# The new keys' value product in a hybrid attention step: one product of 256 columns for two samples instead of one of 128 for each

## The reference

```
# per sample b: 16 queries x 8 heads = 128 query rows, 128 cached + 16 new latent keys of width 512
s = (q_lat @ ckv.T + q_rope @ krope.T) * (128 + 64) ** -0.5     # all_ckv = concat(past, new)
p = softmax(s)
o_lat = p @ ckv                                                 # 128 x 512: the value product
o_a = o_lat (per head) @ w_uv.T
```

## Time and profile before

| | us |
|---|---|
| median of 3 runs (892.14 to 892.81) | 892.15 |
| profiled execution | 892.28 |
| its span | 890.4 |
| TensorE busy (matmuls) | 866.2 |
| TensorE weight loads (beside the matmuls) | 766.4 |
| VectorE, ScalarE, POOL busy | 437.8, 342.3, 125.8 |

### The profile page before, as it was taken

One profiled execution on the slowest core, in us unless ns is written; L12 is line 12 of the kernel. 1 busy time (PEld: TensorE's weight loads), 2 busy tenths in 40 slices (PEclk: granted clock), 3 DMA queues, 4 the chain that ended last, 5 costly groups with the idle time before them and its releaser, 6 DMA issues.

```text
span 890.4 us, 14063 instructions
## 1 busy us (share of the span) xinstructions
PE 866.2 (97%) x5684; PEld 766.4 (86%) x5684; DVE 437.8 (49%) x903; ACT 342.3 (38%) x634; POOL 125.8 (14%) x207
## 2 busy tenths in 40 slices
PE   3999999999999999999999999999999999999996
PEld 2777778899999988888899989988989998888886
DVE  3524442344744224453455467364465566687272
ACT  5423343244453223422333353332244436554252
POOL 0000003110210000103241300000312123630000
PEclk9999999999999999999999999999999999999998
DMA  9999966855544243447463576555898833894313
GB/s 370 413 413 417 379 241 215 254 195 165 153 147 140 92 148 113 135 157 251 144 200 113 159 280 251 213 190 190 273 324 282 270 102 109 324 267 138 123 60 130
DMA packets 50640, 190.07 MB, mean 213 GB/s; under 512 B 7664, under 2 KB 8296, under 8 KB 45328
## 3 DMA queue, kind: packets, MB, share of 16 engines
q1 hardware_dynamic: 35568, 141.61, 44.8%
q0 software_dynamic: 14864, 47.30, 16.5%
q10 hardware_dynamic: 144, 0.26, 0.1%
HBM read 178.55 MB, written 12.69 MB: 215 GB/s over the span
## 4 chain that ended last, share of the span: by engine, by line
PE 90%; DVE 3%; DMA 3%; ACT 2%; issue 1%; SPq 0%; ACTq 0%; DVEq 0%
PE proj L2049 34%; PE proj L2039 30%; DMA araw<-in_ada_pairs 3%; PE bankO L2020 2%; PE proj L2090 2%; PE bankS L2049 2%; PE proj L2020 2%; PE bankT L2049 2%; PE bankO L2171 1%; PE bankS L2090 1%; PE bankO L2183 1%; PE bankO L2258 1%; PE bankS L2240 1%; PE bankO L2269 1%; PE bankS L2039 1%
## 5 line engine op out<-in xcount | busy, mean ns | idle before, releaser
L1465 DVE TENSOR_TENSOR w_lo<-raw,w_hi 128x1024 fp32r<-128x1024 f32 (+3 forms) x166 | 196.2, 1186 | 209.3 <-ACT w_hi L1076 208.1
L1076 ACT ACTIVATE w_hi<-raw 128x1024 fp32r<-128x1024 f32 (+3 forms) x168 | 168.6, 1006 | 179.9 <-PE proj L2039 93.7
L2049 PE MATMUL proj<-hT_hi,w_hi 128*128 128x384 f32 x576 | 198.0, 344 | 0.0
L2049 PE MATMUL proj<-hT_hi,w_lo 128*128 128x384 f32 x576 | 193.3, 336 | 0.0
L2049 PE MATMUL proj<-hT_lo,w_hi 128*128 128x384 f32 x576 | 193.0, 335 | 0.0
L2039 PE MATMUL proj<-w_hi,hT_hi 128*128 128x512 f32 (+2 forms) x458 | 174.5, 381 | 1.2 <-DVE hT_lo L1543 0.9
L2039 PE MATMUL proj<-w_hi,hT_lo 128*128 128x512 f32 (+2 forms) x458 | 171.5, 374 | 0.0
L2039 PE MATMUL proj<-w_lo,hT_hi 128*128 128x512 f32 (+2 forms) x458 | 171.2, 374 | 0.0
L2049 PEld LDWEIGHTS proj<-hT_hi,w_hi 128*128 128x128 f32 x576 | 108.3, 188 | 8.6 <-issue 7.4
L2049 PEld LDWEIGHTS proj<-hT_lo,w_hi 128*128 128x128 f32 x576 | 108.3, 188 | 0.1
L2049 PEld LDWEIGHTS proj<-hT_hi,w_lo 128*128 128x128 f32 x576 | 108.2, 188 | 0.0
(11 more groups left out here) (399 smaller groups left out, 1178.8 us busy)
## 6 DMA issues: line engine op xcount, KB each, us to landing
raw<-in_units SPq DMA_DIRECT2D x181, 512.0 KB, 4.1
araw<-in_ada_pairs SPq DMA_DIRECT2D x32, 1024.0 KB, 8.6
wuvT<-in_w_uv_t POOLq DMA_DIRECT2D x8, 512.0 KB, 6.5
kcT<-in_dsa_k_t POOLq DMA_DIRECT2D x8, 512.0 KB, 6.1
vc<-in_cache_dsa_v POOLq DMA_DIRECT2D x8, 512.0 KB, 5.3
gate_scratch<-stage POOLq DMA_DIRECT2D x8, 384.0 KB, 4.1
raw<-in_units SPq DMA_DIRECT2D x8, 336.0 KB, 3.7
raw<-in_units SPq DMA_DIRECT2D x8, 320.0 KB, 4.8
```

The lines of the kernel that those rows point to most:

```text
L1076: return nc.scalar.activation(out, in_, func, scale=scale, **kw)
L1465: V.tensor_tensor(w_lo[:, SLOT[u], 0:w], raw_of(u)[:, 0:w], high(u)[:, 0:w].bitcast(F32), ALU.subtract).then_inc(lo_ready, 1)
L2049: ins = mm(banks[blk][:, 0:TOK], w[:, n, cols], a[:, kt, :], start=first and n == m == 0, stop=final and n == per - 1 and m == 2)
```

## The change

Samples are taken in pairs. `cnew` now holds the new keys of two samples in each group of 32 rows (12 transfers of 64 KB instead of 24 of 32 KB), and a sample's probabilities of new keys are written to the upper or lower 16 of the 32 columns. `cnx` is done once per pair. A value step `so(n)` takes two of the four column blocks for both samples of pair n // 2; for each block one product of `cnew_r` with 256 columns, and then the cached keys' products of the two samples with 128 columns each. The buffers `pnew_r` and `probsT` hold four samples. The rows of the plan change: `st`, `ss` and `sp` come one unit earlier; `so(n)` stands in unit 149 + n, as before; `cnx(p)` stands first in its row, in units 148, 151, 153 and 155; the loop has 12 rows from unit 145 instead of 11 from 146.

```diff
-    put(u + 1, ("st", 0))
-    u += 2
-    for n in range(DB + 3):
+    put(u, ("st", 0))
+    u += 1
+    for n in range(DB + 4):
+        if n == 3 or n >= 6 and n % 2 == 0 and n // 2 - 2 < DB // 2:
+            put(u + n, ("cnx", max(n // 2 - 2, 0)))
         if n == 1 or 3 <= n < DB + 2:
             put(u + n, ("sp", max(n - 2, 0)))
-        if n >= 3:
-            put(u + n, ("so", n - 3))
+        if n >= 4:
+            put(u + n, ("so", n - 4))
         if n == 0 or 2 <= n <= DB:
             put(u + n, ("ss", max(n - 1, 0)))
         if 1 <= n < DB:
             put(u + n, ("st", n))
-        if 2 <= n < DB + 2:
-            put(u + n, ("cnx", n - 2))
         if n + 2 < DB:
             put(u + n + (n > 0), ("ld_ckT", n + 2))
-        if n < DB:
-            put(u + n + (n > 0), ("ld_cn", n))
-        if n + 3 < DB:
-            put(u + n + (n > 0), ("ld_ck", n + 3))
-    u += DB + 3
+        if n < 2 or n in (6, 8):
+            put(u + n, ("ld_cn", n if n < 2 else n // 2 - 1))
+        if n == 0:
+            put(u, ("ld_ck", 3))
+        if n in (6, 8):
+            put(u + n, ("ld_ck", n - 2), ("ld_ck", n - 1))
+    u += DB + 4
...
-        def cnx(b):
-            act.wait_ge(sem(f"cnew_in{b % 2}"), 48 * (b // 2 + 1))
-            if b:
-                filled(act, "so", b - 1)
-            copy(cnew_r[:], cnew[:, b % 2, :]).then_inc(sem("cnew_rounded"), 1)
+        def cnx(p):
+            act.wait_ge(sem(f"cnew_in{p % 2}"), 48 * (p // 2 + 1))
+            if p:
+                filled(act, "so", 2 * p - 1)
+            copy(cnew_r[:], cnew[:, p % 2, :]).then_inc(sem("cnew_rounded"), 1)
...
-        def so(b):
+        def so(n):
...
-            pe.wait_ge(free["T"], USES["sp", b, "T"] + 1)
-            pe.wait_ge(sem(f"ckvc_in{b % 4}"), 16 * (b // 4 + 1))
-            pe.wait_ge(sem("cnew_split"), b + 1)
-            out = take("so", b, "O")
-            for q in range(CB):
-                cols = slice(P * q, P * (q + 1))
-                mm(out[:, cols], ckvc[:, b % 4, cols], probsT[:, b % 2, 0:P], start=True, stop=False)
-                ins = mm(out[:, cols], cnew_r[:, cols], pnew_r[:, b % 2, :], start=False, stop=True)
+            p, two = n // 2, (n // 2 * 2, n // 2 * 2 + 1)
+            if n % 2 == 0:
+                pe.wait_ge(free["T"], USES["sp", two[1], "T"] + 1)
+                for b in two:
+                    pe.wait_ge(sem(f"ckvc_in{b % 4}"), 16 * (b // 4 + 1))
+                pe.wait_ge(sem("cnew_split"), p + 1)
+            out = take("so", n, "O")
+            new = pnew_r[:, 2 * (p % 2):2 * (p % 2) + 2, :].rearrange("p b q -> p (b q)")
+            for m in range(2):
+                cols = slice(P * (2 * (n % 2) + m), P * (2 * (n % 2) + m + 1))
+                mm(out[:, SEQ * m:SEQ * (m + 1)], cnew_r[:, cols], new, start=True, stop=False)
+                for e, b in enumerate(two):
+                    own = out[:, SEQ * m + P * e:SEQ * m + P * (e + 1)]
+                    ins = mm(own, ckvc[:, b % 4, cols], sample_probsT(b), start=False, stop=e == 1)
             ins.then_inc(full["O"], 1)
```

More of the change, by code:

```diff
@@ L632, in program @@
     cnew, cnew_r = at("cnew", 24, [P, 2, LORA]), at("cnew_r", 94, [P, LORA], F32R)
-    pnew_r = at("pnew_r", 96, [P, 2, P], F32R)
+    pnew_r = at("pnew_r", 37, [P, 4, P], F32R)
     ckvcT = at("ckvcT", 62, [P, 3, CB, NKEY])
@@ L645, in program, with sample_probsT @@
     rls = at("rls", 70, [P, 4, 2, NKEY])
+    def sample_probsT(b):
+        return probsT[:, b % 2, P * (b // 2 % 2):P * (b // 2 % 2 + 1)]
     osq = at("osq", 62, [P, 2, TOK])
@@ L928, in ld_ck, with ld_cn @@
             if b >= 4:
-                filled(pool, "so", b - 4)
+                filled(pool, "so", (b - 4) // 2 * 2 + 1)
             load(ckvc[:, b % 4, :], i["cache_mla_ckv"][0, b], f"ckvc_in{b % 4}")
-        def ld_cn(b):
-            if b == 0:
+        def ld_cn(p):
+            if p == 0:
                 pool.wait_ge(sem("cnew_zero"), 1)
-            if b >= 2:
-                filled(pool, "so", b - 2)
+            if p >= 2:
+                filled(pool, "so", 2 * p - 3)
             for g in range(3):
-                load(cnew[32 * g:32 * g + DS, b % 2, :], o["ckv_s"][0, b], f"cnew_in{b % 2}")
+                load(cnew[32 * g:32 * (g + 1), p % 2, :], o["ckv_s"][0, 2 * p:2 * p + 2].rearrange("b t c -> (b t) c"),
+                     f"cnew_in{p % 2}")
         def ld_kic(_):
@@ L1298, in sp @@
             filled(act, "sp", b, "T")
-            copy(probsT[:, b % 2, 0:P], bank["T"][:, P:2 * P])
-            copy(pnew_r[:, b % 2, :], bank["T"][:, 2 * P:3 * P]).then_inc(sem("pnew_hi"), 1)
-        def cnx(b):
-            act.wait_ge(sem(f"cnew_in{b % 2}"), 48 * (b // 2 + 1))
-            if b:
-                filled(act, "so", b - 1)
-            copy(cnew_r[:], cnew[:, b % 2, :]).then_inc(sem("cnew_rounded"), 1)
+            copy(sample_probsT(b), bank["T"][:, P:2 * P])
+            copy(pnew_r[:, b % 4, :], bank["T"][:, 2 * P:3 * P]).then_inc(sem("pnew_hi"), 1)
+        def cnx(p):
[3 more added lines that the diff above has]
+            copy(cnew_r[:], cnew[:, p % 2, :]).then_inc(sem("cnew_rounded"), 1)
         def dsp(b):
@@ L1705, in sample_max @@
             if kind == "ss":
-                V.tensor_scalar(probs[:, e, 2 * P:2 * P + 96].rearrange("p (g s) -> p g s", s=32)[:, :, 0:DS],
+                V.tensor_scalar(probs[:, e, 2 * P:2 * P + 96].rearrange("p (g s) -> p g s", s=32)[:, :, DS * e:DS * (e + 1)],
                                 probs[:, e, P:NKEY].unsqueeze(1).broadcast_to([P, 3, DS]), scale, None, ALU.mult)
@@ L1722, in sp, with cnx @@
             dve.wait_ge(sem("pnew_hi"), b + 1)
-            low = pnew_r[32:64, b % 2, :]
+            low = pnew_r[32:64, b % 4, :]
             V.tensor_tensor(low, bank["T"][32:64, 2 * P:3 * P], low.bitcast(F32), ALU.subtract).then_inc(free["T"], 1)
-        def cnx(b):
-            dve.wait_ge(sem("cnew_rounded"), b + 1)
-            V.tensor_tensor(cnew_r[64:P, :], cnew[64:P, b % 2, :], cnew_r[64:P, :].bitcast(F32),
+        def cnx(p):
+            dve.wait_ge(sem("cnew_rounded"), p + 1)
+            V.tensor_tensor(cnew_r[64:P, :], cnew[64:P, p % 2, :], cnew_r[64:P, :].bitcast(F32),
                             ALU.subtract).then_inc(sem("cnew_split"), 1)
-        def so(b):
-            filled(dve, "so", b, "O")
-            V.tensor_copy(qlT[:, :, b, :], bank["O"][:].rearrange("p (k q) -> p k q", k=CB)).then_inc(free["O"], 1)
+        def so(n):
+            filled(dve, "so", n, "O")
+            p, q = n // 2, 2 * (n % 2)
+            V.tensor_copy(qlT[:, q:q + 2, 2 * p:2 * p + 2, :].rearrange("p k b q -> p k (b q)"),
+                          bank["O"][:].rearrange("p (k q) -> p k q", k=2)).then_inc(free["O"], 1)
         def oa(n):
```

## The result

| | before | after |
|---|---|---|
| median of 7 runs, us | 892.28 | 895.38 |
| lowest to highest | 892.14 to 892.81 | 895.07 to 895.55 |
| span of the profiled execution | 890.4 | 893.4 |

The changed kernel is slower: ratio 1.0032, 95% interval 1.0023 to 1.0042, or 3.1 us. Predicted were 893.6 us in a range from 892.6 to 896.0, with 895.4 us as the price of the rival in which the clock falls. The range held the time; the likeliest case was not the one that came.

What follows compares the result with a forecast made beforehand. TensorE, busy 866.2 of 890.4 us, was taken as the bound. Saved work of 1.4 us against a 2.8 us stall gave +1.4 us, with 0.13 us off for the median: 893.6 us, range 892.6 to 896.0.

Steps and rivals of the forecast that it cites:

- the rival in which the clock falls: TensorE's clock drops to its lower level in unit 151's stall, costing 1.8 us more: 895.4 us; chance 0.30.
- the likeliest case: TensorE stalls in unit 151 and its clock stays up: 893.6 us, own range 893.1 to 894.2; chance 0.50.
- The wait: Unit 151: pair 1's value step waits for evictions, then `cnx` on ScalarE and VectorE; TensorE stalls 2.83 us.
- The stated upper bound, 3.2 us: Longest stall allowed for at unit 151, with three handoffs between engines of 0.2 us each.
- The saved work: TensorE's eight value steps save 1.6 us through fewer passes, less 0.2 us for row edges: 1.4 us net.
- The price of 0.120 us for a pass of 256 columns: New-key product in the value step, priced from the prompt's fp32r key products; bounds 0.111 to 0.215 us.
- The two signs: In TensorE's timeline, 256-column passes would show a pitch of 0.12 us and value steps would take 1.1 us.
- Forecast (stall, clock holds): 0.50: Unit 151's stall comes but TensorE's clock keeps its upper level; own range 893.1 to 894.2 us, chance 0.50.
- the share of 41%: Part of TensorE's time taken as lost at the lower clock, from transposes at 16.16 and 19.36 us.
- The argument against a fall: The clock's fall at the kernel's end came with nothing following, and unit 151's stall is hardly longer.
- The sum: Whole kernel: -1.4 us of TensorE work and +2.8 us of stall give +1.4 us, so 893.6 us.
- The other `cnx` places: Units 153 and 155: no wait expected, with some 0.3 us to spare at pair 2, over 1 us at pair 3.

Runs made afterwards that it cites:

- experiment 5: The kernel before, without pairing, with `cnx` of sample 2 moved from the end of unit 150's row to the front of unit 151's: 897.14 us.
- experiment 6: The changed kernel with `cnx` at the end of the row before its value step, and loads for pairs 2 and 3 one row earlier: 890.93 us.
- experiments 2: The changed kernel with `cnx` in the row before its value step and each 256-column product split into two of 128 columns: 892.66 us.
- experiment 4: The changed kernel with the scores of sample 5 ahead of the value step in unit 151's row instead of behind it: 892.55 us.
- experiment 3: The changed kernel with 12 products of `ones` that feed nothing put ahead of TensorE's wait for pair 1 in unit 151: 893.83 us.

## Why the prediction was right, and where not
**The wait.** Right in place, cause and order, a little small: 455.47 against the 452.34 of an undelayed start (0.03 us behind the last transpose) is 3.13 us, predicted 2.83. The handoff from VectorE to TensorE was taken as 0.06 us and measured 455.47 - (454.52 + 0.69) = 0.26 us; it was 0.26 us in experiment 5 as well. The rest is that the new step, undelayed, starts 0.1 us closer behind the transposes (0.03 us for 0.11 us). The stated upper bound, 3.2 us, had allowed 0.2 us for each handoff.

**The saved work.** Right in the sum. TensorE's net gain was put at 1.4 us; experiment 6 against before has 82.00 - 80.39 = 1.61 us in the traces and 1.48 us in the medians. A regular row shortened from 465.16 - 458.20 = 6.96 us to 477.18 - 470.44 = 6.74 us. The price of 0.120 us for a pass of 256 columns, read off another step, held as a difference: the 1.67 us between experiments 2 and 6 are 0.104 us for each of 16 dropped passes, and 2 x 0.111 - 0.104 = 0.118 us. The two signs that the prediction named for it did not come as named. A value step takes 1.21 us, not 1.1 us, and from the start of a wide pass to the next pass it is 439.15 - 438.95 = 0.20 us; its first block takes 439.52 - 438.95 = 0.57 us, as worked out (0.564 us), its second one 440.16 - 439.52 = 0.64 us up to the scores. The gain is whole all the same, since the step starts 0.08 us sooner behind the transposes and the scores behind it take 0.06 us less (441.29 - 440.16 = 1.13 us for 460.89 - 459.70 = 1.19 us).

**The clock.** This is the step that failed: "Forecast (stall, clock holds): 0.50". The clock fell, which had 0.30. Its price had been put at 1.8 us and is 1.6 us: 0.75 us on the value step and 0.9 us on the scores. The lower level lasted 3.4 us here and 3.4 us in experiment 5, where the prediction had 2 to 5 us. It had read the pace at 16.16 us as that level; the granted clock of that moment, in the trace of before, does not say so:
```profile
16.00:17.00 1.00, 1.00 (x11) 0.84 (x5) 0.00 (x0) 1.00 (x2) 0.00 (x0) 1.00 1.08 451
```
So the share of 41% came from a stretch for which the trace does not show the lower level. Behind the stall, where it does, 38% of the value step's time and 44% of the scores' were lost: the figure was right, without that row having shown it. The argument against a fall was that the one at the kernel's end came with nothing following; but the fall came here even though work had already resumed. The end of the wait did not save the clock. The Trainium skill's section on why this matters for your kernels (TensorE: Matmul & The Clock Gate) puts the harmful gap a little higher than this one; here the clock fell already with 2.9 us of idling, in two kernels, and held with 1.7 us, in one. What lies between was not tried.

One moment of the record was also too little to go by. The prediction took 2.4 us between TensorE's last product and the fall from the end of before. The same distance, read at the end of each trace in the same way, differs from kernel to kernel; the shortest is in experiment 4, the longest in experiment 5:
```profile
883.90 0.28 PE L2101 MATMUL bankT<-w_hx,hT_lo 128*128 128x256 f32 x1
...
886.00:887.00 1.00, 0.00 (x0) 0.00 (x0) 0.90 (x3) 0.77 (x3) 0.00 (x0) 0.58 0.00 0
```
```profile
887.79 0.28 PE L2092 MATMUL bankT<-w_hx,hT_lo 128*128 128x256 f32 x1
...
892.00:893.00 1.00, 0.00 (x0) 0.00 (x0) 0.00 (x0) 0.00 (x0) 0.00 (x0) 0.52 1.05 381
```
From the means of 0.58 and 0.52, a fall from 1.00 to 0.50 lies at 886.16, 2.0 us behind the last product's end at 884.18, and at 892.04, 4.0 us behind 888.07. The changed kernel has 3.1 us there. In the two stalls the fall came 3.2 us (455.81, the last transpose ends at 452.58) and 3.5 us (455.14, 451.63) after TensorE had stopped.

**The sum.** -1.6 + 3.1 + 1.6 = +3.1 us, against 3.16 us in the traces and 3.10 us in the medians. That the rival's 895.4 us hit the measured 895.38 us is partly luck: it had 0.2 us too little saved, 0.3 us too little wait and 0.2 us too much for the clock. The range held because the rival's case had been taken into it; the forecast itself, 893.6 us, was 1.8 us too low.

**The rest.** The other `cnx` places caused no wait, as predicted for pairs 2 and 3; at pair 2 VectorE was done at 470.22, 0.35 us ahead of the value step, where 0.3 us had been worked out. The late transfer for pair 2 was not seen ahead; it cost nothing in the changed kernel. The pairing at its best is worth 0.17%. The prediction called anything under 0.2% hard to tell from none; the interval of experiment 6, 0.9974 to 0.9992, leaves out no change, if barely.

## What to carry to other kernels
When a step moves from the end of one row to the front of the next, look at what each engine does between the two: here an eviction that waits for the very unit in front of which the step is needed. On a full TensorE, price a new wait of about 3 us at one and a half times its length (here 3.1 us and 1.6 us on top), since the clock may fall behind it, and first look for work that can be done inside it. If a change to a full engine saves less than a percent, check its waits before the idea is given up: here the idea brought 1.6 us, and one row of the schedule lost 4.7 us.

## What was not expected of the hardware
The granted clock falls after TensorE has resumed: 0.3 us after in the changed kernel (resumed 455.47, fell 455.8), and 0.6 us after in experiment 5 (resumed 454.52, fell 455.14). From TensorE's last product to the fall it took anything from 2.0 to 4.0 us in eight traces, so one reading of it gives no limit for a harmless wait. While at 1.2 GHz, a value step took 1.96 instead of 1.21 us and a score step 2.02 instead of 1.14 us. The handoff from VectorE to a TensorE idle for 1.7 to 2.9 us took 0.26 us in two kernels and 456.25 - (455.30 + 0.69) = 0.26 us in experiment 4, against 0.06 us after an idle time of 0.26 us and 0.05 us in experiment 3, where the same two instructions meet and TensorE is kept busy up to the handoff.
